# Prompt scores over 128 contraction rows: stacked key halves and doubled queries instead of four fp32 corner products

## The chip, the cores and the metric

The kernel runs on one core of one Trainium2 chip. The metric is the device time of one execution in microseconds (us), the median of several runs. Smaller is better.

## The reference, cut to what matters

One layer of a decoder: input projection, sparse attention with three branches (compressed, selected, window), a gated MLP branch, two merge projections and an output projection, for 512 prompt tokens and 8 x 4 sample tokens. The change touches the attention of the prompt. For 512 tokens all 8 selection blocks fit in the 16 that are picked and the window covers the prompt, so the selected and the window branch are both plain causal attention, each with its own keys and values:

```python
q5 = q.reshape(B, Tq, KV_HEADS, HPG, dh) * (dh ** -0.5)       # 2 key groups, 4 heads each, dh = 64
s = jnp.einsum('bqgjd,bcgd->bgjqc', q5, kc); p = masked_softmax(s, cend <= qpos)     # compressed, 31 blocks
s = jnp.einsum('bqgjd,bgqnkd->bgjqnk', q5, kg); p = masked_softmax(s, msel)          # selected
s = jnp.einsum('bqgjd,bkgd->bgjqk', q5, kw);    p = masked_softmax(s, mw)            # window
```

## The kernel before, in words

Every engine walks one common list, ORDER, written out by `plan()`, and does its own part of each entry; nothing is reordered at run time. An entry that waits holds up all later entries of that engine. SyncE (SP) and GpSimd (POOL) walk the list too and issue most DMAs.

The large projections are entries "main": one group is 24 matmuls of 128 rows by 272 or 256 columns (line 1729), three fp32r passes over 8 blocks of rows (high by high, high by low, low by high). Weights arrive in halves of a slot (`raw`); ScalarE rounds them to `w_hi` ("split", line 1046), VectorE subtracts for `w_lo` ("low", line 1313), and SP then loads the next half.

Prompt attention takes 16 units: token tile i in the order 3, 2, 1, 0 (128 queries, 128(i+1) keys: 512, 384, 256, 128 columns), branch y, and a pair of head rows jh. A unit is worked as:
- "ps" (line 2028, TensorE): scores, in two halves jj. Each half fills two banks (one for each key group g) with four fp32 matmuls of 64 rows by 64 columns of weights, one in each corner of the array. In the trace each fp32 matmul is two records, so a half is 8 records. There are three score banks.
- "ps" on VectorE (line 1611): mask and maximum of each bank.
- "px" (line 1211, ScalarE): exp; "pn" (lines 1621 and 1624 on VectorE, 1220 on ScalarE): weights and scaling; "tt" (line 1635): VectorE transposes in 32-blocks into `p_turn`, and 16 DMAs move the blocks into place, 7 issued by SP (line 837), 9 by GpSimd (line 1002).
- "pp" (line 2037): products with the values.

Beside the units, for each tile k of the compressed branch, come "cs" (line 2000, TensorE scores from `qT` and `kcp`; line 1578, VectorE), "cx", "cn", "ct" (line 2007) and "cv" (line 2014). "cs k+1" comes at the end of unit 4k+1. Between all of these stand main groups, one to a half unit. After unit 15 only projections are left, with the final norm.

Earlier in the list: the queries and keys of the prompt are turned into `qT` and `kT` ("qT", "kT", about 70 to 99 us); at 109 to 204 us the compression network; at 213 to 286 us the sample tokens' attention (`qkS`, `s_max` and so on), which uses `q_bd` and a key buffer `turned_late`.

Of the kernel before, what the change touches and what calls it, by code (L numbers as in the profile page):

```python
# [161 lines left out]
def rows_of(s):  # L162

    return ("main", s, NT, 0)
# [7 lines left out]
def plan():  # L172
# [98 lines left out]
    for c in range(1, NCH):  # L271
# [17 lines left out]
            order.append(("ln2", 0 if c == 4 else 3))  # L289
        order += ([s] if c != 7 else []) + [x for x in after if x not in (("ln", NT), ("lnr",))] + extra.get(c, [])  # L290
        turn(2)
    order += [("hidl", NCH - 1)]

    def keys(q, first, count):
        order.extend(("kt", q, k) for k in range(first, first + count))
# [5 lines left out]
    main(1)  # L301
    keys(0, 7, 5)
    main(2)
    order += [("qkS", 0)]
    for q in range(NQ):
        for n, step in enumerate(("s_max", "s_turn", "s_imp", "s_mask", "s_exp", "s_scale")):
            if step == "s_scale":
                continue
            order += [(step, q)]
            if q == 0 and n in (1, 2):  # L310
                keys(1, 3 * n - 3, 3)
            if step == "s_exp":
# [24 lines left out]

    def products(u):
        order.extend(("pp", u, kt) for kt in range(units[u][0] + 1))

    order += [("cx", 0)]
    for u in range(len(units)):
        n, k = u % 4, u // 4
        order += [("ps", u, 0)]
# [163 lines left out]
def nsa_gmlp_layer(nc, x_p, x_s, ck_cmp, cv_cmp, ck_sel, cv_sel, ck_win, cv_win, pages, w_in, w1k, w1v, w_sp,  # L508
                   w_pa, w_pb, w_o, norm_g, final_g, params, consts, outs):
    (y_p, y_s, pk_cmp, pv_cmp, pk_sel, pv_sel, pk_win, pv_win,  # L510
     sk_cmp, sv_cmp, sk_sel, sv_sel, sk_win, sv_win, s_chunk) = outs
    ctx = ExitStack()
    with ctx:
        def sb(name, shape, dt=F32):
# [2 lines left out]
        def sem(name):  # L517
            return ctx.enter_context(nc.semaphore(name))
# [40 lines left out]
        kT = placed("kT", 2048, [P, 2, TP])  # L559
        v_tok = placed("v_tok", 4096, [P, 2, NT + 1, P])  # L560
        U = placed("U", 5376, [P, 13832])
        x_hi, x_lo = placed("x_hi", 0, [P, 8, T], F32R), placed("x_lo", 4352, [P, 8, T], F32R)
# [51 lines left out]
        def sig_at(b, d):  # L614
# [51 lines left out]
        p_scored, p_bias, p_masked, p_exp, p_scaled = (sem("p_scored"), sem("p_bias"), sem("p_masked"), sem("p_exp"),  # L666
                                                       sem("p_scaled"))
        mix_ready = sem("mix_ready")
        m_sum, m_hi, m_lo = sem("m_sum"), sem("m_hi"), sem("m_lo")
        f_ssq, f_ms, f_root, f_out = sem("f_ssq"), sem("f_ms"), sem("f_root"), sem("f_out")  # L670
        f_inv, f_part, f_sum, f_out_act = sem("f_inv"), sem("f_part"), sem("f_sum"), sem("f_out_act")
# [96 lines left out]
        def _(sp):  # L768
# [43 lines left out]
            for s in ORDER:  # L812
# [7 lines left out]
                elif s == ("xt", 2, 0):  # L820
                    wait_evacuated(sp, T_AT[("qTs",)])
                    for f in range(4):
                        for a in range(4):
                            sp.dma_start(q_quarters[32 * a:32 * a + 32, f, :, :], q_bd[32 * f:32 * f + 32, :, :]).then_inc(q_spread, 16)
                elif s[0] == "load_w1":
                    sp.dma_start(w1_at[0], w1k).then_inc(w1_loaded[0], 16)
                    sp.dma_start(w1_at[1], w1v).then_inc(w1_loaded[1], 16)
                elif s[0] == "xt" and s[2] == 0 and s[1] % 5 in (1, 3):

                    for b in range(2 * n_win, 2 * n_win + 2):  # L830
                        sp.dma_start(sk_win[b, 0:512 - TQ, :], ck_win[b, TQ:512, :]).then_inc(win_out, 16)
                        sp.dma_start(sv_win[b, 0:512 - TQ, :], cv_win[b, TQ:512, :]).then_inc(win_out, 16)
                    n_win += 1
                elif s[0] == "tt" and moves_with(s[1]) == s[1]:
                    sp.wait_ge(p_turned, s[1] + 1)
                    for n in range(BY_SYNC):
                        sp.dma_start(*block_move(s[1], n)).then_inc(p_moved[s[1] % 4], 16)
                elif s[0] == "oz" and s[1] == NT - 1:

                    sp.wait_ge(p_used, len(UNITS))  # L840
                    sp.dma_start(xr[0][:, :], x_p[tok(0), :]).then_inc(xr_loaded[0], 16)
                    for j in range(4):
                        sp.dma_start(x_rows[32 * j:32 * j + 32, :, :], in_quarters(x_s)[:, j, :, :]).then_inc(xr_loaded[NT], 16)
                    sp.dma_start(pm("final_g"), final_g).then_inc(fg_loaded, 16)
                elif s[0] == "load_x":
                    i = s[1]
                    sp.wait_ge(m_lo, (4, 8, 14)[i - 1])
                    sp.dma_start(xr[i][:, :], x_p[tok(i), :]).then_inc(xr_loaded[i], 16)
                elif s[0] == "fin":
                    i = s[1]  # L850
                    k = FINS.index(i)
                    if i == NT:
                        sp.wait_ge(f_out, k + 1)
                        for j in range(4):
                            sp.dma_start(in_quarters(y_s)[:, j, :, :], x_rows[32 * j:32 * j + 32, :, :]).then_inc(y_out, 16)
# [10 lines left out]
        def _(pool):  # L866
# [97 lines left out]
            for s in ORDER:  # L964
# [7 lines left out]
                elif s[0] == "rope":  # L972
# [12 lines left out]
                    else:  # L985
                        g = s[1] - 2
                        wait_main_read(pool, last_of(f"A{g}"))
                        rope_all(512, J, G, g)
                elif s == ("ln2", NT):
                    pool.wait_ge(vn_ready, NT + 1)  # L990
                    pool.dma_start(s_chunk, vg[0:TS, NT, :]).then_inc(out_done, 16)
# [26 lines left out]
        def _(act):  # L1018
            for s in ORDER:
# [180 lines left out]
                elif kind == "ct" and t_uses(s) == ["act"]:  # L1200
                    act.wait_ge(t_done, t + 1)
                    if s[1]:
                        act.wait_ge(c_used, G * s[1])
                    nc.scalar.copy(ctb[s[2]][0:NCP, :], TB[t % 2][0:NCP, :]).then_inc(t_act, 1)
                elif kind == "px":
                    u = s[1]
                    n = (UNITS[u][0] + 1) * P
# [41 lines left out]
        def _(dve):  # L1249
# [24 lines left out]
            for s in ORDER:  # L1274
# [350 lines left out]
                elif kind == "tt":  # L1625
# [10 lines left out]
                    ins.then_inc(p_turned, 1)  # L1636
                elif kind == "oz":
                    i = TILES[s[1]]
                    dve.wait_ge(p_used, 4 * (s[1] + 1))
# [80 lines left out]
        def _(pe):  # L1720
# [11 lines left out]
            for s in ORDER:  # L1732
# [260 lines left out]
                    pe.transpose(tb[:, 0:P], o_row[:, :], ident).then_inc(t_done, 1)  # L1993
                elif kind == "cs":
                    i = TILES[s[1]]
                    if s[1] == 0:
                        wait_evacuated(pe, T_AT[("qT", NT - 1)])
                        wait_evacuated(pe, T_AT[("kT", 1)])
                    for j in range(J):
                        ins = mm(tb[:, j * 2 * NCP:(j + 1) * 2 * NCP].rearrange("p (g n) -> p g n", g=G), qT[:, j, tok(i)], kcp[:, :, :], start=True, stop=True)  # L2000
                    ins.then_inc(t_done, 1)
                elif kind == "ct":
                    i, g = s[1], s[2]
# [12 lines left out]
                elif kind == "ps":  # L2016
                    u, jj = s[1], s[2]
                    i, y, jh = UNITS[u]
                    n = (i + 1) * P
                    if u == 0 and jj == 0:  # L2020
                        pe.wait_ge(s_exp, NQ)
                    for c in range(2):
                        for g in range(G):
                            k = J * u + 2 * jj + g
                            if k >= 3 and c == 0:
                                pe.wait_ge(p_masked, k - 2)
                            r, q = slice(64 * g, 64 * g + 64), slice(i * P + 64 * c, i * P + 64 * c + 64)
                            ins = mm(S[k % 3][64 * c:64 * c + 64, 0:n], qT[r, 2 * jh + jj, q], kT[r, y, 0:n], start=True, stop=True)  # L2028
                            if c:
                                ins.then_inc(p_scored, 1)  # L2030
                elif kind == "pp":
                    u, k = s[1], s[2]
                    i, y, jh = UNITS[u]
# [71 lines left out]
```

## Time and profile before

| | us |
|---|---|
| median of 3 runs (541.36 to 541.96) | 541.64 |
| profiled execution, whole | 543.01 |
| its span in the trace | 541.3 |
| TensorE busy in the span | 523.7 (97%) |
| VectorE / ScalarE / GpSimd busy | 331.2 / 243.1 / 157.0 |

The profile is of one execution; its own time is 1.4 us above the median. A busy share is an average over stages. A matmul's duration holds its passage through the array, which overlaps with the next one, so costs on TensorE are read from start to start.

### The profile page before, as it was taken

The numbers are of one execution on the slowest core, as the hardware profiler recorded it, in microseconds if no ns is written. First come the engines' busy times: TensorE is split into PE (matmuls) and PEld (weight loads), VectorE is DVE, ScalarE is ACT, GpSimd is POOL, SyncE is SP. The second block draws the span as 40 slices with busy tenths as digits, with TensorE's granted clock in tenths as the row PEclk, the third lists the DMA queues.
The fourth block names the chain that finished last, engine by engine and source line by source line (L and its number), as shares of the span: only waits on it lengthen the run. The fifth ranks groups of instructions, "written<-read, shape, count | busy, mean of one in ns | idle before, by whom it ended". The sixth has DMA issues, their size and how long they took to land.

```text
span 541.3 us, 12831 instructions
## 1 busy us (share of the span) xinstructions
PE 523.7 (97%) x5198; PEld 473.3 (87%) x5198; DVE 331.2 (61%) x838; ACT 243.1 (45%) x564; POOL 157.0 (29%) x257
## 2 busy tenths in 40 slices
PE   6899999999999999999989999999999999999995
PEld 4899999999999998987978766767779999999995
DVE  4723231388898765674564678687753477763565
ACT  6543424534533323241241887677674432323334
POOL 0006933044414633734000066473453000000000
PEclk9999999999999999999999999999999999999998
DMA  8527652448525465877331267563454435306104
GB/s 296 214 82 218 235 181 80 154 141 290 173 61 195 142 198 168 264 282 238 101 97 40 79 155 186 148 155 100 128 140 125 131 114 155 119 1 196 40 7 161
DMA packets 59789, 81.05 MB, mean 150 GB/s; under 512 B 7825, under 2 KB 49233, under 8 KB 59218
## 3 DMA queue, kind: packets, MB, share of 16 engines
q1 hardware_dynamic: 48320, 49.97, 30.4%
q0 software_dynamic: 10688, 29.14, 17.6%
q10 hardware_dynamic: 722, 1.12, 0.6%
q8 instruction: 41, 0.67, 0.5%
q14 instruction: 18, 0.15, 0.1%
HBM read 65.23 MB, written 8.13 MB: 136 GB/s over the span
## 4 chain that ended last, share of the span: by engine, by line
PE 91%; DVE 3%; issue 2%; ACT 1%; DMA 1%; POOL 1%; DVEq 0%
PE m L1729 62%; PE so L2028 4%; PE so L2037 3%; PE so L1900 3%; PE so L1903 3%; PE so L1901 3%; PE m L1813 2%; PE so L1939 2%; PE so L1877 1%; PE so L1988 1%; DMA U<-p_turn 1%; PE t L1865 1%; POOL U L1002 1%; PE t L1755 1%; PE so L1742 1%
## 5 line engine op out<-in xcount | busy, mean ns | idle before, releaser
L1729 PE MATMUL m<-h_hi,w_hi 128*128 128x272 f32 x448 | 132.7, 296 | 1.0 <-DVE za L1426 0.8
L1729 PE MATMUL m<-h_hi,w_lo 128*128 128x272 f32 x448 | 129.2, 288 | 0.0
L1729 PE MATMUL m<-h_lo,w_hi 128*128 128x272 f32 x448 | 128.7, 287 | 0.0
L1729 PE MATMUL m<-w_hi,h_hi 128*128 128x256 f32 (+2 forms) x360 | 104.1, 289 | 2.4 <-issue 1.9
L1729 PE MATMUL m<-w_hi,h_lo 128*128 128x256 f32 (+2 forms) x360 | 101.9, 283 | 0.0
L1729 PE MATMUL m<-w_lo,h_hi 128*128 128x256 f32 (+2 forms) x360 | 101.9, 283 | 0.0
L1313 DVE TENSOR_TENSOR w_lo<-raw,w_hi 128x1024 fp32r<-128x1024 f32 (+2 forms) x62 | 71.0, 1155 | 42.6 <-ACT w_hi L1046 42.5
L1729 PEld LDWEIGHTS m<-h_hi,w_hi 128*128 128x128 f32 x448 | 84.3, 188 | 13.4 <-issue 10.2
L1002 POOL DMA_DIRECT2D U<-p_turn x108 | 58.2, 547 | 104.0 <-DVE p_turn L1635 102.6
L1729 PEld LDWEIGHTS m<-h_hi,w_lo 128*128 128x128 f32 x448 | 84.5, 189 | 0.0
L1729 PEld LDWEIGHTS m<-h_lo,w_hi 128*128 128x128 f32 x448 | 84.4, 188 | 0.0
L1729 PEld LDWEIGHTS m<-w_hi,h_hi 128*128 128x128 f32 (+1 forms) x360 | 67.8, 188 | 3.9 <-issue 2.1
L1729 PEld LDWEIGHTS m<-w_lo,h_hi 128*128 128x128 f32 (+1 forms) x360 | 68.0, 189 | 0.1
L1729 PEld LDWEIGHTS m<-w_hi,h_lo 128*128 128x128 f32 (+1 forms) x360 | 67.8, 188 | 0.1
L1046 ACT CAST w_hi<-raw 128x1024 fp32r<-128x1024 f32 (+2 forms) x62 | 60.9, 990 | 1.0 <-DMA raw<-in_w_in 0.5
L1611 DVE CUSTOM_DVE_ANT_0 U<-so,cst 128x512 f32<-128x512 f32 (+3 forms) x64 | 28.7, 485 | 20.2 <-PE so L2028 20.2
L1220 ACT ACTIVATE U<-U,st 128x512 f32<-128x512 f32 (+3 forms) x64 | 30.7, 551 | 18.9 <-DVE st L1624 18.9
L1729 PE MATMUL m<-x_hi,w_lo 128*128 128x272 f32 x128 | 37.0, 289 | 0.0
L1729 PE MATMUL m<-x_hi,w_hi 128*128 128x272 f32 x128 | 36.8, 288 | 0.0
L1729 PE MATMUL m<-x_lo,w_hi 128*128 128x272 f32 x128 | 36.7, 287 | 0.0
L1211 ACT ACTIVATE U<-U,st 128x512 f32<-128x512 f32 (+3 forms) x64 | 35.1, 551 | 2.9 <-DVE st L1615 2.9
L1900 PE MATMUL so<-xt_sb,w_hi 128*128 128x256 f32 x128 | 32.0, 290 | 0.2 <-ACT xt_sb L1161 0.2
(301 smaller groups left out, 904.3 us busy)
## 6 DMA issues: line engine op xcount, KB each, us to landing
raw<-in_w_in SPq DMA_DIRECT2D x36, 512.0 KB
U<-in_x_p SPq DMA_DIRECT2D x8, 512.0 KB, 5.9
raw<-in_w_o SPq DMA_DIRECT2D x8, 512.0 KB
U<-p_turn POOLq DMA_DIRECT2D x54, 64.0 KB, 2.6
U<-p_turn SPq DMA_DIRECT2D x42, 64.0 KB, 2.8
raw<-in_w_in SPq DMA_DIRECT2D x8, 256.0 KB
raw<-in_w_pa SPq DMA_DIRECT2D x8, 256.0 KB
raw<-in_w_pb SPq DMA_DIRECT2D x4, 512.0 KB
```

The lines of the kernel that those rows point to most:

```text
L1002: pool.dma_start(*block_move(s[1], n)).then_inc(p_moved_pool[s[1] % 4], 16)
L1046: ins = nc.scalar.copy(hi, x)
L1211: ins = nc.scalar.activation(pb[u][:, j, 0:n], pb[u][:, j, 0:n], ACT.Exp, bias=st[:, m + 4 + j:m + 5 + j], scale=SCALE, accum_out=st[:, m ...
L1220: ins = nc.scalar.activation(pb[u][:, j, 0:n], pb[u][:, j, 0:n], ACT.Copy, scale=st[:, m + 12 + j:m + 13 + j])
L1313: ins = v.tensor_tensor(lo, x, hi.bitcast(F32), ALU.subtract)
L1611: v.tensor_tensor_reduce(pb[u][:, a, 0:n], S[k % 3][:, 0:n], cs("causal")[:, 512 - n:512], 1.0, -3e38, ALU.add, ALU.max, st[:, m + a:m + a ...
L1729: ins = mm(out, lhs(a, k), rhs(b, k), start=(k == 0 and a + b == 0), stop=(k == n - 1 and a == 1))
L1900: mm(out[:, 0:256], w, x(xt_hi), start=(j == 0), stop=False, skip_group_check=True)
L1901: ins = mm(out[:, 0:256], w1_lo[:, j, :], x(xt_hi), start=False, stop=False, skip_group_check=True)
L1903: ins = mm(out[:, 0:256], w, x(xt_lo), start=False, stop=(j == 15), skip_group_check=True)
L2028: ins = mm(S[k % 3][64 * c:64 * c + 64, 0:n], qT[r, 2 * jh + jj, q], kT[r, y, 0:n], start=True, stop=True)
L2037: ins = mm(O[64 * g:64 * g + 64, 256 * jh:256 * jh + 256].rearrange("p (j a r) -> p j a r", j=2, a=4), v_tok[:, y, k, g * DH:(g + 1) * DH] ...
```

## The change

The high part (fp32r rounding) and the low part (remainder) of the keys are stacked to 128 rows in `k_st`: for group g the high part on rows 64g to 64g+63, the low part on the other 64. The queries are stored on both halves of the partitions ("doubled"), split into `q_h` and `q_l`, and each bank of scores is made by two full-array fp32r matmuls, 128 rows by 128 queries, over 128(i+1) key columns. `k_st` lies where `qT` was, so the queries go out to DRAM (`q_dram`) and come back for each pair of units; `cs` reads its plain queries back too, into `h_rows` and `q_bd`. New entries of the list:
- "ks": ScalarE two copies, VectorE two subtractions (64 x 1024), GpSimd two DMAs, ahead of "hidl 9".
- "ql m": ScalarE issues two DMAs for unit pair m. "qh m": ScalarE copies 128 x 512, VectorE subtracts 128 x 512.
- "qc k": GpSimd issues four DMAs of 64 KB for `cs k`.

The order of units within a tile becomes head pair outside, branch inside. The core of the diff:

```diff
-    order += [("hidl", NCH - 1)]
+    order += [("ks",), ("hidl", NCH - 1)]
...
-    order += [("qkS", 0)]
+    order += [("ql", 0), ("qkS", 0)]
...
+            if q == NQ - 1 and n == 0:
+                order += [("qc", 0)]
...
-            order += [("s_out", q), ("qkS", 1)]
+            order += [("s_out", q), ("qkS", 1), ("qh", 0)]
...
-    units = [(i, y, jh) for i in TILES for y in range(2) for jh in range(2)]
+    units = [(i, y, jh) for i in TILES for jh in range(2) for y in range(2)]
...
-    order += [("cx", 0)]
+    order += [("ql", 1), ("cx", 0)]
...
         if u:
             order += [("pn", u - 1)]
+            if u % 2 and m < len(units) // 2:
+                order += [("qh", m)]
...
             order += [("ct", k, 0), ("ct", k, 1)]
+            if k < NT - 1:
+                order += [("qc", k + 1)]
         order += [("px", u)]
+        if u % 2 and m + 1 < len(units) // 2:
+            order += [("ql", m + 1)]
...
+                elif s[0] == "qTs":
+                    for i in range(NT):
+                        wait_evacuated(sp, T_AT[("qT", i)])
+                    for g in range(G):
+                        sp.dma_start(q_dram[:, :, g, :], qT[64 * g:64 * g + 64, :, :]).then_inc(q_saved, 16)
...
+                elif s[0] == "qc":
+                    i = TILES[s[1]]
+                    if s[1]:
+                        pool.wait_ge(t_done, T_AT[("cs", s[1] - 1)] + 1)
+                    else:
+                        pool.wait_ge(qk_done, NQ)
...
+                    for n in range(2):
+                        for g in range(G):
+                            pool.dma_start(q_plain[n][64 * g:64 * g + 64, :, :], q_dram[:, 2 * n:2 * n + 2, g, tok(i)]).then_inc(q_plain_loaded, 16)
+                elif s[0] == "ks":
+                    pool.wait_ge(k_lo_done, 1)
+                    for g in range(G):
+                        a, b = slice(64 * g, 64 * g + 64), slice(64 - 64 * g, 128 - 64 * g)
+                        pool.dma_start(k_st[b, g, :, :], k_lo[a, :, :]).then_inc(k_moved, 16)
...
+                elif kind == "ql":
...
+                    for a in (slice(0, 64), slice(64, 128)):
+                        nc.scalar.dma_start(q_f[m % 2][a, :, :], src).then_inc(q_loaded[m % 2], 16)
+                elif kind == "qh":
+                    m = s[1]
+                    act.wait_ge(q_loaded[m % 2], 32 * (m // 2 + 1))
+                    nc.scalar.copy(q_h[m % 2][:, :, :], q_f[m % 2][:, :, :]).then_inc(q_hi_done, 1)
...
+                elif kind == "qh":
+                    m = s[1]
+                    dve.wait_ge(q_hi_done, m + 1)
+                    v.tensor_tensor(q_l[m % 2][:, :, :], q_f[m % 2][:, :, :], q_h[m % 2][:, :, :].bitcast(F32), ALU.subtract).then_inc(q_lo_done, 1)
...
-                    for c in range(2):
-                        for g in range(G):
-                            k = J * u + 2 * jj + g
-                            if k >= 3 and c == 0:
-                                pe.wait_ge(p_masked, k - 2)
-                            r, q = slice(64 * g, 64 * g + 64), slice(i * P + 64 * c, i * P + 64 * c + 64)
-                            ins = mm(S[k % 3][64 * c:64 * c + 64, 0:n], qT[r, 2 * jh + jj, q], kT[r, y, 0:n], start=True, stop=True)
-                            if c:
-                                ins.then_inc(p_scored, 1)
+                    for g in range(G):
+                        k = J * u + 2 * jj + g
+                        if k >= 3:
+                            pe.wait_ge(p_masked, k - 2)
+                        for x in (q_h, q_l):
+                            ins = mm(S[k % 3][:, 0:n], x[m % 2][:, 2 * jj + g, :], k_st[:, g, y, 0:n], start=(x is q_h), stop=(x is q_l))
+                        ins.then_inc(p_scored, 1)
```

## Rows read from the trace of the kernel before

**Rows 1.** The page, busy time: us, share of the span, instructions.
```profile
PE 523.7 (97%) x5198; PEld 473.3 (87%) x5198; DVE 331.2 (61%) x838; ACT 243.1 (45%) x564; POOL 157.0 (29%) x257
```

**Rows 2.** Windows, 312 to 344 us: stretch, us, busy by engine PE, PEld, DVE, ACT, POOL.
```profile
312.00:344.00 32.00, 31.98 (x242) 21.89 (x241) 23.63 (x67) 24.15 (x54) 20.16 (x38) 1.00 0.66 168
```

**Rows 3.** Timeline of TensorE, 302.6 to 304.1 us: start, us.
```profile
302.63 0.29 PE L1729 MATMUL m<-h_hi,w_lo 128*128 128x272 f32 x1
302.85 1.09 PE L2028 MATMUL so<-kT,qT 64*64 64x512 f32 x8
303.87 0.39 PE L1729 MATMUL m<-h_hi,w_hi 128*128 128x272 f32 x1
304.10 0.29 PE L1729 MATMUL m<-h_lo,w_hi 128*128 128x272 f32 x1
```

**Rows 4.** Chain of work that ended last: start, us, what, records.
```profile
307.16 0.84 PE t L2000 x8
...
333.70 0.81 PE so L2028 x8
...
391.13 0.38 PE so L2028 x8
...
420.83 66.14 PE m L1729 x528
...
520.52 14.37 PE m L1729 x120
```

**Rows 5.** Timelines of VectorE, ScalarE and GpSimd; idle time before each in brackets.
```profile
200.80 0.47 ACT L1173 ACTIVATE U<-so,prm 128x256 f32<-128x256 f32 x1 [6.27 <-PE so L1903]
...
204.16 0.44 DVE L1413 TENSOR_TENSOR sg<-sg,tmp 128x272 f32<-128x272 f32 x1 [3.87 <-issue]
...
255.78 0.22 DVE L1492 TENSOR_REDUCE st<-so 128x1 f32<-128x63 f32 x1 [2.69 <-PE so L1946]
...
200.98 0.94 POOL L943 DMA_INDIRECT turned_late<-in_ck_sel,half_rows  x1 [7.02 <-PE so L1903]
```

**Rows 6.** Timelines of VectorE and ScalarE, unit 1, and two like operations.
```profile
191.81 1.89 DVE L1450 TENSOR_TENSOR xt_sb<-U,xt_sb 128x512 fp32r<-128x512 f32 x3
...
302.73 0.17 DVE L1624 TENSOR_TENSOR st<-st,gate 128x4 f32<-128x4 f32 x1
302.81 1.22 DVE L1313 TENSOR_TENSOR w_lo<-raw,w_hi 128x1024 fp32r<-128x1024 f32 x1
...
307.88 2.48 DVE L1635 STREAM_TRANSPOSE p_turn<-U 128x512 f32<-128x512 f32 x4
310.29 0.38 DVE L1578 TENSOR_TENSOR U<-t,cst 128x248 f32<-128x248 f32 x1
...
311.48 0.68 DVE L1611 CUSTOM_DVE_ANT_0 U<-so,cst 128x512 f32<-128x512 f32 x1
...
238.75 0.60 ACT L1196 COPY U<-t 128x512 f32<-128x512 f32 x1
...
302.93 2.56 ACT L1220 ACTIVATE U<-U,st 128x512 f32<-128x512 f32 x4 [0.45 <-DVE st L1624]
```

**Rows 7.** Chain, scores of units 2 and 3.
```profile
312.23 1.86 PE so L2028 x10
```

**Rows 8.** Timeline of GpSimd: issues of the block moves after unit 3 and unit 7.
```profile
335.00 4.87 POOL L1002 DMA_DIRECT2D U<-p_turn  x9 [1.75 <-DVE p_turn L1635]
...
366.26 4.84 POOL L1002 DMA_DIRECT2D U<-p_turn  x9 [1.74 <-DVE p_turn L1635]
```

**Rows 9.** Line 1002: time from a move's issue to its landing.
```profile
DMA to landing us min/median/max: 1.7/2.3/5.7
```

**Rows 10.** Chain, the compressed scores of tiles 2 and 3.
```profile
343.63 1.03 PE t L2000 x8
...
371.30 1.03 PE t L2000 x8
```

**Rows 11.** Windows near the end: busy by engine, granted clock, DMA share, GB/s.
```profile
537.00:538.00 1.00, 0.00 (x0) 0.00 (x0) 0.93 (x4) 0.69 (x1) 0.00 (x0) 0.50 0.70 260
```

More of the change, by code:

```diff
@@ L339, in products @@
         order.extend(("pp", u, kt) for kt in range(units[u][0] + 1))
-    order += [("cx", 0)]
+    order += [("ql", 1), ("cx", 0)]
     for u in range(len(units)):
         n, k = u % 4, u // 4
+        m = u // 2 + 1
         order += [("ps", u, 0)]
@@ L511, in nsa_gmlp_layer @@
      sk_cmp, sv_cmp, sk_sel, sv_sel, sk_win, sv_win, s_chunk) = outs
+    q_dram = nc.dram_tensor("q_dram", (DH, J, G, TP), F32, kind="Internal").ap()
     ctx = ExitStack()
@@ L559, in nsa_gmlp_layer @@
         kT = placed("kT", 2048, [P, 2, TP])
+        k_st = placed("k_st", 0, [P, G, 2, TP], F32R)
+        k_lo = placed("k_lo", 2048, [P, 2, TP], F32R)
+        q_f = [placed(f"q_f{n}", 2048 + 1024 * n, [P, J, P]) for n in range(2)]
+        q_l = [placed(f"q_l{n}", 2048 + 1024 * n, [P, J, P], F32R) for n in range(2)]
+        q_h = [placed(f"q_h{n}", 2560 + 1024 * n, [P, J, P], F32R) for n in range(2)]
+        q_plain = [x[:, :, :].rearrange("p k t -> p (k t)").rearrange("p (j n) -> p j n", j=2) for x in (h_rows, q_bd)]
         v_tok = placed("v_tok", 4096, [P, 2, NT + 1, P])
@@ L668, in nsa_gmlp_layer @@
         mix_ready = sem("mix_ready")
+        q_saved, k_hi_done, k_lo_done, k_moved = sem("q_saved"), sem("k_hi_done"), sem("k_lo_done"), sem("k_moved")
+        q_loaded, q_hi_done, q_lo_done = [sem("q_loaded0"), sem("q_loaded1")], sem("q_hi_done"), sem("q_lo_done")
+        q_plain_loaded = sem("q_plain_loaded")
         m_sum, m_hi, m_lo = sem("m_sum"), sem("m_hi"), sem("m_lo")
@@ L988, in _ @@
                         rope_all(512, J, G, g)
+                elif s[0] == "qc":
[4 more added lines that the diff above has]
+                        pool.wait_ge(qk_done, NQ)
+                        pool.wait_ge(main_done, MAIN_AT[rows_of(SLOT["V1"])] + 1)
+                        pool.wait_ge(q_saved, 32)
+                    for n in range(2):
[6 more added lines that the diff above has]
+                        pool.dma_start(k_st[b, g, :, :], k_lo[a, :, :]).then_inc(k_moved, 16)
                 elif s == ("ln2", NT):
@@ L1204, in _ @@
                     nc.scalar.copy(ctb[s[2]][0:NCP, :], TB[t % 2][0:NCP, :]).then_inc(t_act, 1)
+                elif kind == "ks":
+                    for y in range(2):
+                        wait_evacuated(act, T_AT[("kT", y)])
+                    act.wait_ge(q_saved, 32)
+                    for g in range(G):
+                        r = slice(64 * g, 64 * g + 64)
+                        ins = nc.scalar.copy(k_st[r, g, :, :], kT[r, :, :])
+                    ins.then_inc(k_hi_done, 1)
+                elif kind == "ql":
+                    m = s[1]
+                    i, _, jh = UNITS[2 * m]
+                    if m == 0:
+                        act.wait_ge(k_moved, 32)
+                    elif m == 1:
+                        act.wait_ge(o_done, NQ)
+                    else:
+                        act.wait_ge(p_scored, 2 * J * (m - 1))
+                    src = q_dram[:, 2 * jh:2 * jh + 2, :, tok(i)].rearrange("d j g t -> d (j g) t")
+                    for a in (slice(0, 64), slice(64, 128)):
[4 more added lines that the diff above has]
+                    nc.scalar.copy(q_h[m % 2][:, :, :], q_f[m % 2][:, :, :]).then_inc(q_hi_done, 1)
                 elif kind == "px":
@@ L1636, in _ @@
                     ins.then_inc(p_turned, 1)
+                elif kind == "ks":
+                    dve.wait_ge(k_hi_done, 1)
+                    for g in range(G):
+                        r = slice(64 * g, 64 * g + 64)
+                        ins = v.tensor_tensor(k_lo[r, :, :], kT[r, :, :], k_st[r, g, :, :].bitcast(F32), ALU.subtract)
+                    ins.then_inc(k_lo_done, 1)
+                elif kind == "qh":
+                    m = s[1]
+                    dve.wait_ge(q_hi_done, m + 1)
+                    v.tensor_tensor(q_l[m % 2][:, :, :], q_f[m % 2][:, :, :], q_h[m % 2][:, :, :].bitcast(F32), ALU.subtract).then_inc(q_lo_done, 1)
                 elif kind == "oz":
@@ L1995, in _ @@
                     i = TILES[s[1]]
-                    if s[1] == 0:
-                        wait_evacuated(pe, T_AT[("qT", NT - 1)])
-                        wait_evacuated(pe, T_AT[("kT", 1)])
+                    pe.wait_ge(q_plain_loaded, 16 * 4 * (s[1] + 1))
                     for j in range(J):
-                        ins = mm(tb[:, j * 2 * NCP:(j + 1) * 2 * NCP].rearrange("p (g n) -> p g n", g=G), qT[:, j, tok(i)], kcp[:, :, :], start=True, stop=True)
+                        ins = mm(tb[:, j * 2 * NCP:(j + 1) * 2 * NCP].rearrange("p (g n) -> p g n", g=G), q_plain[j // 2][:, j % 2, :], kcp[:, :, :], start=True, stop=True)
                     ins.then_inc(t_done, 1)
@@ L2019, in _ @@
                     n = (i + 1) * P
+                    m = u // 2
                     if u == 0 and jj == 0:
                         pe.wait_ge(s_exp, NQ)
-                    for c in range(2):
-                        for g in range(G):
-                            k = J * u + 2 * jj + g
-                            if k >= 3 and c == 0:
-                                pe.wait_ge(p_masked, k - 2)
-                            r, q = slice(64 * g, 64 * g + 64), slice(i * P + 64 * c, i * P + 64 * c + 64)
-                            ins = mm(S[k % 3][64 * c:64 * c + 64, 0:n], qT[r, 2 * jh + jj, q], kT[r, y, 0:n], start=True, stop=True)
-                            if c:
-                                ins.then_inc(p_scored, 1)
+                        pe.wait_ge(k_moved, 32)
+                    if u % 2 == 0 and jj == 0:
+                        pe.wait_ge(q_hi_done, m + 1)
+                        pe.wait_ge(q_lo_done, m + 1)
+                    for g in range(G):
+                        k = J * u + 2 * jj + g
[4 more added lines that the diff above has]
+                        ins.then_inc(p_scored, 1)
                 elif kind == "pp":
```

## The prediction

> **What bounds the kernel now.** I read the page's busy shares first: TensorE is busy 97% of the span, the next engine 61% [rows 1]. Then windows over the stage of the prompt scores: of the 32 us from 312 TensorE is busy 31.98, VectorE 23.63, ScalarE 24.15, GpSimd 20.16 [rows 2]. So what is taken from TensorE's queue here shortens the run, and every wait put into that queue lengthens it by its full length: after unit 15 it has only projections, 528 matmuls in a row in 66.14 us [rows 4], in which nothing can be made up. But VectorE and ScalarE have only about a quarter of their time left, and both work their lists strictly in order. The chain shows that they do bind once already: a stretch of scores takes 1.86 us [rows 7] where 10 records at 1.02 us for 8 would take 1.3. So the next views were the timelines of VectorE, ScalarE and GpSimd between 286 and 409 us, entry by entry against ORDER.
>
> **TensorE's own work.** A half unit of 512 columns takes 1.02 us from its start (302.85) to the next main group's (303.87); 384 columns take 0.81 and 128 take 0.38 [rows 3, 4]. That is 1.67 ns per column, four cycles of 2.4 GHz for all four corners together, plus 0.17; 256 columns give 0.59. Around it, the matmul before starts 0.22 ahead of it instead of 0.125, and the first main matmul after it holds 0.23 instead of 0.125 [rows 3, 4]: 0.10 us to enter the cornered form and 0.11 to leave it.
> Afterwards a half is four full-array fp32r matmuls. Main matmuls of 272 columns come every 66.14/528 = 125.3 ns [rows 4], which is 113.3 of columns plus 12. So 512 columns: 4 x (213.3 + 12) = 0.90 us; 384: 0.69; 256: 0.48. The streaming is the same four cycles per column as before; only the fixed parts differ. For 128 columns no row has an fp32r matmul so narrow. Lower end: 4 x (53.3 + 12) = 0.26. Upper end: the fp32 rate of four cycles per column, 4 x 213 = 0.85. The nearest row in shape is a full-array weight load with 62 columns behind it, 0.84 us for 8 records, 105 ns each [rows 4], so 0.43 is taken.
> Eight halves of each width: 8 x (-0.12 - 0.12 - 0.11 + 0.05) = -2.4 us. By ORDER, 20 halves are entered from a full-array neighbour and 23 left to one: 20 x 0.10 + 23 x 0.11 = 4.5 us gone. In their place 10 are now entered from a cornered or half-width neighbour ("pp", "cv", the sample values) and 7 left to one: 1.8 us new. Sum -5.1 us; with the ends of the 128-column price -6.4 to -1.7.
> On these borders a rule of the Trainium skill bears, page "TensorEngine Tiling (Array Packing)", section "Key Properties": changing the tiling mode drains TensorE, changing the tile within a mode does not. The trace agrees (0.22 against 0.125). By the page alone, whose tiles multiply throughput, giving up four concurrent 64 x 64 tiles should cost; by the rows it costs nothing, since fp32r needs a quarter of fp32's cycles. Without the drains the sum would be -2.4.
>
> **Parts ahead of the stage: nothing.** "ks": ScalarE's two copies and VectorE's two subtractions of 64 x 1024, about 1.1 us each, fall ahead of 200.80 and 204.16, where these engines sat idle 6.27 and 3.87 us; GpSimd's two DMAs fall in its idle 7.02 us [rows 5]. Without that cover the sample keys would come late and TensorE would wait up to 4 us before the sample scores. "qh 0": VectorE has 2.69 us idle ahead of 255.78 [rows 5], the subtraction takes 0.63. Storing the queries (1 MB) puts SP's later loads back by some 3 us at about 103 us, where they are prefetches. "ql 0" and "qc 0" have over 20 us each until their use. I keep 0, with up to +1 for the range.
>
> **The query split in the odd units.** "qh m" stands right behind "pn" of the even unit. On ScalarE that means behind the four scalings, 302.93 to 305.49 in unit 1, then its own copy, 0.6 us [rows 6]: done at 306.0. VectorE meets "qh 1" at 302.9, directly after its last weight operation, and can't pass it: it stands for 3.1 us and then needs 0.63 (three like subtractions take 1.89) [rows 6]. Behind it in VectorE's queue stand, in this order, a "low", two masks, a second "low", the transposes of unit 0, "cs 1" and the masks of unit 2, for which TensorE waits through its three score banks. From 306.6: low 1.2, masks 1.3 (0.68 each, less an overlap), bias 0.2, low 1.2, transposes 2.4, cs 1.2 [rows 6] give 314.1 for the first mask of unit 2 instead of 311.48, 2.6 us late, done at 314.7. The last bank of unit 2 needs that mask; TensorE is there at about 312.0 and stands 2.5 us. "qh 2" in unit 3 does the same again. Walking the four queues through units 2 to 4 in this way, with each entry's own duration, I get 5.8 us of TensorE waits where the same walk of the kernel before has 1.4: +4.4 us. The walk of the kernel before reaches the last product of the stage within 0.3 us of the trace. Later ones (units 5 to 13) mostly find VectorE ahead, because of the next item; they add 1.2 us around unit 8 and 1.3 us around units 12 to 14. ScalarE's 14 extra issues and 7 copies are inside this walk. Bounds: 0 if VectorE had its work done, and 7 x 3.7 = 26 if nothing hid any.
>
> **The reload for the compressed scores.** "qc 2" stands in GpSimd's queue behind the nine block moves after unit 3, "qc 3" behind the nine after unit 7. TensorE's "cs 2" and "cs 3" now wait for them; before they waited for nothing. In the timing before, the moves after unit 7 are issued from 366.26 to 371.10 [rows 8]. Four more issues at 0.54 each: the last starts at 372.7 and lands 2.3 us later (the median of the moves) [rows 8, 9], at 375.0. TensorE reaches "cs 3" at 371.30 [rows 10], and about 0.7 us earlier relative to unit 8 by its own savings: a wait of some 4.4 us. For "cs 2" likewise: moves 335.00 to 339.87, landing at 343.8, TensorE at 343.63 [rows 8 to 10]: 1 us. To this comes that the transposes which release the moves sit late on VectorE through "qh": in the walk by 1.5 us more at either place, giving 2.7 and 6.0 us, 8.7 together. All that stands behind "cs" on TensorE waits too, the main groups among it. Bounds: 5.4 if VectorE isn't late; 8.7 + 2 x 3 = 15 if both landings take the longest of the moves, 5.7 us [rows 9].
>
> **Sum.** -5.1 + 4.4 + 1.2 + 1.3 + 8.7 = +10.5 us on an execution of 543.0, 553.5; the runs shown have their median 1.4 lower, so 552.0.
>
> **Rivals.**
> (a) Only the work saved counts: both reloads land in time and VectorE takes the splits in its gaps. Then -5.1, less about 1 us because VectorE already binds at units 2 and 3: 537.5, faster. For it: VectorE is idle a quarter of the stage. Against it: the idle time lies behind entries that wait for TensorE, and GpSimd's 4.84 us of issues ahead of "qc 3" are in the trace.
> (b) One of the two waits only. Without the "qh" effect the walk gives +3.5, without the "qc" effect +4: 545. It decides if the copies on ScalarE come earlier than I think, or if TensorE has enough ahead of "cs".
> (c) TensorE's clock falls in the 6 us wait. At the end of the run its last group ends at 534.9 [rows 4], and the window from 537 shows 0.50, that is 1.2 GHz [rows 11]. So a gap like that before "cs 3" is long enough. If 3 to 5 us of work follow at half clock, +1.5 to +2.5: 554. The Trainium skill's page "TensorE: Matmul & The Clock Gate", section "Part 1: The HAM clock gate", says that idleness halves the clock and that renewed work restores it; the first half agrees with the trace, the way back no row shows.
> (d) 128 columns run at the upper end, 8 x 0.42 = +3.4: 555.
>
> **How the numbers follow.** My sum 0.45, (b) 0.20, (c) 0.13, (d) 0.10, (a) 0.12. The likeliest gives 552.0. (a) lies on the faster side, and with it comes a strip of (b): faster 0.12, same 0.03, slower 0.85, where about 0.2% is what this kernel's runs can tell from no change. The range leaves out (a) and the far end of the landings: 543.5 to 558.
>
> **What would show it.** Right: TensorE waits of 4 to 7 us ahead of line 2000 in tile 0 or 1's compressed scores, released by a DMA that GpSimd issued; VectorE idle some 3 us before each subtraction of the queries, released by ScalarE; halves of 512 columns at 0.90 us; main groups of 3.01 us next to them. Wrong: "cs" with no wait, or TensorE over 96% busy between 286 and 421 us; a wait near 204 to 214 us for `k_moved` or late keys would mean that I mis-priced "ks".

## The result, and the profile after

| | before | after |
|---|---|---|
| median, us (4 runs each) | 541.55 (541.36 to 541.96) | 561.59 (561.30 to 563.53) |
| ratio to before, 95% interval | 1 | 1.036 (1.033 to 1.039) |
| profiled execution / its span | 543.01 / 541.3 | 561.73 / 560.0 |
| prompt attention: start of the first score to start of the last product group | 286.26 to 419.82 = 133.6 | 287.70 to 438.52 = 150.8 |

The change costs 3.6%, 20 us. The forecast was 552.0 us with a range to 558: the direction and the two causes of waiting were right, the size was not.

Of the 18.7 us between the two spans, 17.2 lie in the prompt attention. The other 1.5 come at 16 to 24 us, long before anything that was changed (told at the end).

The page after; this line answers to [rows 1]:

```profile
PE 528.7 (94%) x5070; PEld 492.7 (88%) x5070; DVE 338.1 (60%) x848; ACT 249.5 (45%) x574; POOL 168.5 (30%) x275
```

TensorE has 128 instructions fewer and is busy 5 us *longer*, at a lower share. Work taken out and yet more busy time: the same work must have run slower. The windows say where: first those of before, then after (columns as in [rows 2], with the granted clock, the DMA share and GB/s last).

```profile
346.00:376.00 30.00, 30.00 (x254) 21.70 (x252) 23.52 (x79) 22.46 (x60) 15.39 (x29) 1.00 0.50 125
376.00:406.00 30.00, 29.15 (x270) 22.02 (x268) 20.71 (x91) 21.97 (x73) 14.35 (x27) 1.00 0.53 138
```

```profile
316.00:346.00 30.00, 29.57 (x204) 24.49 (x205) 22.15 (x63) 24.25 (x54) 19.04 (x36) 0.94 0.69 181
346.00:376.00 30.00, 25.96 (x181) 21.44 (x178) 20.55 (x61) 18.80 (x51) 15.61 (x30) 0.94 0.58 142
376.00:406.00 30.00, 22.22 (x141) 19.43 (x140) 17.18 (x65) 16.16 (x47) 12.06 (x22) 0.83 0.50 123
```

Two things are new: TensorE stands (22.22 of 30 us where it was 29.15), and its clock is below 1.00 in these three windows. From 284 to 316 and from 406 to 436 us it is 1.00, and before in all five. The clock has two levels, 1.2 and 2.4 GHz, so a mean of 0.83 over 30 us is a third of the time at the lower one. What was lost to it is (1 - clock) x length: (0.06 + 0.06 + 0.17) x 30 = 8.7 us. Up to 0.8 of it cost nothing: from 384.00 to 385.85 the clock is 0.58 while TensorE still waits.

TensorE's waits between 286 and 440 us, by what ended them (us in total, times, longest). Before, to the end of its stage, then after:

```profile
PE so L2037 <- DMA U<-p_turn: 0.6, 1, 0.6
PE so L2028 <- DVE st L1611: 0.2, 1, 0.2
```

```profile
PE t L2072 <- DMA q_bd<-q_dram: 9.9, 2, 6.6
PE so L2104 <- DVE st L1675: 4.7, 6, 1.9
PE so L2112 <- DMA U<-p_turn: 0.3, 1, 0.3
PE so L2104 <- issue: 0.2, 1, 0.2
```

15.1 us against 0.8. The first line is the reload of `cs`, the second the masks of the score banks. Both are in the chain of work that ended last. Around unit 1 it now runs through ScalarE and VectorE; before, through TensorE [rows 7]:

```profile
304.66 1.93 ACT U L1284 x3
306.59 0.52 ACT q_h L1268
307.13 0.69 DVE q_l L1710
307.83 1.13 DVE w_lo L1377
...
311.51 2.40 DVE p_turn L1699 x4
...
315.02 0.68 DVE U L1675
```

ScalarE's scalings, its copy of the queries, VectorE's subtraction, everything queued behind that, and only at 315.02 the mask that TensorE's third bank needs; before it was at 311.48 [rows 6]. The timelines of VectorE and TensorE show the wait at either end (idle time in brackets):

```profile
307.13 0.69 DVE L1710 TENSOR_TENSOR q_l<-q_f,q_h 128x512 fp32r<-128x512 f32 x1 [3.14 <-ACT q_h L1268]
```

```profile
315.77 0.58 PE L2104 MATMUL so<-k_st,q_h 128*128 128x512 f32 x1 [1.93 <-DVE st L1675]
```

And the chain around `cs 3`, which before was entered from TensorE's own work at 371.30 [rows 10]:

```profile
378.44 2.70 POOL U L1042 x5
381.13 1.17 POOL h_rows L1023 x2
382.30 0.56 POOL q_bd L1023
382.87 2.85 DMA q_bd<-q_dram
...
385.85 1.94 PE t L2072 x8
387.79 0.96 PE so L2104 x4
388.75 4.13 PE m L1803 x24
```

Block moves, four more issues behind them, the landing, then TensorE. Now read durations: the eight records of `cs` take 1.94 us where they took 1.03, and a main group of 24 matmuls 4.13 where it takes 3.01 at full clock. That is work at 1.2 GHz after the wait, for the greater part of both. In windows of 4 us:

```profile
380.00:384.00 4.00, 0.00 (x0) 0.00 (x0) 2.31 (x10) 2.67 (x9) 3.46 (x7) 1.00 0.71 164
384.00:388.00 4.00, 2.15 (x10) 2.18 (x11) 0.17 (x1) 0.00 (x0) 0.00 (x0) 0.54 0.21 41
388.00:392.00 4.00, 4.00 (x23) 4.00 (x23) 3.15 (x10) 1.71 (x4) 0.00 (x0) 0.61 0.00 0
```

But the long waits are not the only ones that cost clock. After the 1.93 us at 315.77 it reads:

```profile
312.00:316.00 4.00, 2.07 (x14) 1.63 (x14) 3.93 (x10) 1.35 (x4) 1.80 (x4) 1.00 0.87 231
316.00:320.00 4.00, 4.00 (x16) 3.12 (x16) 2.73 (x11) 3.35 (x6) 3.11 (x6) 0.57 0.79 194
```

TensorE is busy throughout the second window and gets 16 records done; in the window after it, at 1.00, 29.

### The profile page after: what moved, and what is told of

Its sections match the earlier page's. It is cut to its first block, busy times and chain, and to the rows that moved or that the text cites. A ratio compares the mean times of both kernels' runs of the same rounds, so it can differ in the third digit from the quotient of the medians.

```text
span 560.0 us, 12647 instructions
## 1 busy us (share of the span) xinstructions
PE 528.7 (94%) x5070; PEld 492.7 (88%) x5070; DVE 338.1 (60%) x848; ACT 249.5 (45%) x574; POOL 168.5 (30%) x275
## 4 chain that ended last, share of the span: by engine, by line
PE 76%; DVE 10%; ACT 5%; POOL 3%; issue 3%; DMA 3%; DVEq 0%
PE m L1803 53%; PE so L1974 3%; PE so L1977 3%; DVE p_turn L1699 3%; PE so L1975 3%; POOL U L1042 3%; ACT U L1284 2%; DVE U L1675 2%; PE m L1887 2%; PE so L2013 1%; DVE w_lo L1377 1%; PE so L2104 1%; PE so L1951 1%; DMA q_bd<-q_dram 1%; PE so L2062 1%
## 5 line engine op out<-in xcount | busy, mean ns | idle before, releaser
L1803 PE MATMUL m<-h_hi,w_lo 128*128 128x272 f32 x448 | 130.4, 291 | 0.0
L1803 PE MATMUL m<-h_lo,w_hi 128*128 128x272 f32 x448 | 130.2, 291 | 0.0
L1803 PEld LDWEIGHTS m<-h_hi,w_hi 128*128 128x128 f32 x448 | 86.1, 192 | 3.7 <-issue 1.8
L1803 PEld LDWEIGHTS m<-h_lo,w_hi 128*128 128x128 f32 x448 | 86.1, 192 | 0.3
L1803 PEld LDWEIGHTS m<-h_hi,w_lo 128*128 128x128 f32 x448 | 85.9, 192 | 0.0
```

The costliest lines, as they stand in the source:

```text
L1803: ins = mm(out, lhs(a, k), rhs(b, k), start=(k == 0 and a + b == 0), stop=(k == n - 1 and a == 1))
```

## The experiments

One theory runs through them: the stage's length is 133.6 us, less 5.1 us for TensorE's own work saved, plus its waits beyond the 0.8 of before, plus what the lower clock takes. The 5.1 is the forecast, not a measurement. What tells the theories apart stands in this table, which the sections below explain (us; stage from first score to last product as above; waits from 284 or 286 us on; clock loss from windows of about 30 us; sum = 128.5 + waits - 0.8 + clock loss, for the three kernels of the old form 133.6 in place of 128.5):

| kernel | ratio to before | waits | clock loss | sum | stage measured |
|---|---|---|---|---|---|
| before | 1 | 0.8 | 0 | 133.6 | 133.6 |
| changed | 1.036 | 15.1 | 8.7 | 151.5 | 150.8 |
| 1 query split early | 1.016 | 10.2 | 5.1 | 143.0 | 142.8 |
| 2 reload early | 1.010 | 6.4 | 4.9 | 139.0 | 139.5 |
| 3 both early | 0.9955 | 2.7 | 0 | 130.4 | 130.8 |
| 4 waits filled (+8.8 of idle work) | 1.026 | 8.2 | 1.8 | 146.5 | 148.2 |
| 5 changed again | 1.031 | 15.9 | 9.9 | 153.5 | 152.6 |
| 6 only the copy early | 0.993 | 2.7 | 0 | 130.4 | 130.6 |
| 7 both early, mains spread | 0.988 | 1.5 | 0 | 129.2 | 128.7 |
| 8 before with a reload wait | 1.009 | 5.2 | 1.5 | 139.5 | 139.6 |
| 9 before, mains spread | 0.997 | 1.0 | 0 | 133.8 | 132.4 |
| 10 as 7, again | 0.991 | 1.2 | 0 | 128.9 | 128.3 |

The sum is off by up to 1.7 us. In 9 it is 1.4 too high, because the list of waits leaves out a stretch in which TensorE counts as busy: the ten records in 1.86 us of [rows 7] become eight in 1.09 when unit 2 has another main group ahead of its mask.

Since the median of the kernel before was 540.6, 544.5 and 542.2 us in the three sets of runs, the ratios are what is to be compared, and beside them the stages of the profiles. The microseconds of whole executions mislead. In the twelve profiles the first score starts anywhere from 283.0 to 288.1 us: from 283.0 to 284.6 in experiments 1 to 4, and at 287.6 and 288.0 in the two of the changed kernel. From the start of the last product group to the end it is the same 121.5 us in all twelve.

### 1. The query split a unit earlier

```diff
-            if u % 2 and m < len(units) // 2:
-                order += [("qh", m)]
...
+        if u % 2 == 0 and m < len(units) // 2:
+            order += [("qh", m)]
         order += [("px", u)]
```

> The query split of pair m stands a unit earlier, ahead of the exp of the even unit, instead of behind its scalings. Theory (queue order, then clock): VectorE no longer stands 3 us for ScalarE in every odd unit; TensorE's waits before scores fall from 4.7 us to about 3, and cs 3 still waits 4 to 5 us for GpSimd's reload. By the walk 7 us less than the changed kernel, by its fewer clock falls some 3 more: 551 to 555 us. Rival (the full-array form itself slows or throttles TensorE): within 2 us of the changed kernel, 560 to 562, clock 0.98 as there.

Measured: 549.12 us (548.73 to 551.72), ratio 1.016 (1.012 to 1.020). Waits for masks fell from 4.7 to 2.5 us, those for the reload from 9.9 to 7.2, since the transposes that release the moves come sooner; the clock loss from 8.7 to 5.1. In the stage that saves 8.0 us, where 7 of walk and some 3 of clock were expected: a wait removed gives its clock back too. That the time lies below my range comes from ahead of the stage, where this execution's first score starts 4.7 us sooner.

### 2. The reload issued right behind the `cs` before it

```diff
-            if k < NT - 1:
-                order += [("qc", k + 1)]
+            if k == 0:
+                order += [("qc", 1)]
...
+            if n == 1 and k < NT - 2:
+                order += [("qc", k + 2)]
```

The first of these stands behind "ct", the second behind "cs k+1".

> The reload for the next compressed scores is issued right behind the ones before it, four units of GpSimd moves earlier; the query split stays. Theory (queue order, then clock): the two waits of TensorE at its compressed scores (3.3 and 6.6 us) are gone, the waits for VectorE stay or grow: by the walk 6.5 us less, with the clock falls behind them 8 to 12 less: 550 to 554 us. Rival (form itself): 560 to 562.

Measured: 546.98 us (545.49 to 547.38), ratio 1.010 (1.007 to 1.013). `cs` waits for nothing any more:

```profile
PE so L2106 <- DVE st L1677: 4.5, 6, 1.9
PE so L2106 <- ACT q_h L1270: 1.9, 1, 1.9
```

The time is below my range for the same reason as in 1; the stage is 11.3 us shorter, where 8 to 12 were expected. But the clock still falls, though no single wait is over 1.94 us. Windows and the waits inside them:

```profile
308.00:312.00 4.00, 2.40 (x18) 1.97 (x16) 3.93 (x9) 1.92 (x6) 1.23 (x3) 1.00 0.91 259
312.00:316.00 4.00, 3.66 (x11) 2.76 (x12) 2.73 (x12) 2.78 (x6) 4.00 (x8) 0.60 0.83 197
```

```profile
312.34 0.50 PE L2106 MATMUL so<-k_st,q_h 128*128 128x512 f32 x1 [1.94 <-DVE st L1677]
...
384.69 0.45 PE L2106 MATMUL so<-k_st,q_h 128*128 128x128 f32 x1 [1.87 <-ACT q_h L1270]
```

At the second place the wait is for ScalarE's copy, and 0.77 us for a mask follow at 386.12. So waits of under 2 us can pull the clock down on their own. They don't always do it: see 5.

### 3. Both

The two edits together.

> Both moves. Theory: no reload wait, VectorE waits about 3 us in all, no clock fall in the stage: the walk gives 3.5 us less than before, 538 us (536 to 541). If only one of the two placements mattered: about that one's time, 550 or more. Rival (form itself slows or throttles): at least 550.

Measured: 538.36 us (537.58 to 539.54, 8 runs), ratio 0.9955 (0.9935 to 0.9975), as expected, and faster than before. The clock is 1.00 in every window from 284 to 436 us, and the waits left are

```profile
PE so L2106 <- DVE st L1677: 2.5, 3, 1.5
PE so L2114 <- DMA U<-p_turn: 0.2, 1, 0.2
```

The arithmetic of the change was good all along; the stage is 2.8 us shorter with 1.9 us more of waits, so TensorE's own work is 4.7 us less. Undoing one delay saves 2.0 or 2.6 points of ratio (8.0 or 11.3 us of the stage), undoing both 4.0 points (20.0 us).

### 4. The waits filled with idle matmuls

The changed kernel, with 22 and 48 matmuls of 272 columns, whose results nobody reads, ahead of the waits of `cs 2` and `cs 3`.

```diff
+                    for _ in range((0, 0, 22, 48)[s[1]]):
+                        mm(tb[:, 0:272], h_hi[:, 0, 0:P], h_hi[:, 1, 0:272], start=True, stop=True)
```

> The changed kernel with TensorE given 22 idle matmuls of 272 columns (2.8 us) ahead of its wait for the reload in cs 2 and 48 (6.0 us) ahead of the one in cs 3; their result is overwritten. More work, all of it inside waits. Theory with the clock: the clock no longer falls after these waits, 3 to 6 us less than the changed kernel (555 to 558). If the clock fall costs nothing, or has another cause: 0 to 1 us more than the changed kernel (561 to 563).

Measured: 554.61 us (554.15 to 556.98), ratio 1.026 (1.022 to 1.030), for 70 matmuls more; the changed kernel has 1.036, and 1.031 (1.027 to 1.035) in experiment 5. The 7 us between the medians overstate the effect: of 6.9 us between the spans (553.1 and 560.0) 4.2 lie ahead of the first score. The stage is 2.7 us shorter. The waits for the reload shrank, the clock came back:

```profile
PE so L2106 <- DVE st L1675: 5.8, 8, 1.9
PE t L2074 <- DMA q_bd<-q_dram: 2.2, 2, 1.3
```

```profile
346.00:376.00 30.00, 28.64 (x212) 23.74 (x213) 21.06 (x68) 19.81 (x50) 17.32 (x33) 1.00 0.57 139
376.00:406.00 30.00, 27.89 (x206) 24.72 (x205) 18.11 (x69) 17.51 (x56) 10.56 (x20) 0.94 0.48 120
```

`cs 3` starts 98.2 us behind the first score with and without the idle work, since it waits for GpSimd either way; what the clock gave back behind `cs 2` was waited away there. From the start of `cs 3` to the last product group it is 49.9 us instead of 52.6. These 2.7 us isolate the clock: no dependency and no transfer was changed. The clock loss is 1.8 us instead of 8.7, but 1.7 of the difference is the fall at 316 us, ahead of the first idle matmul (342.3); the same wait of 1.94 us stands here at 311.56 and the clock stays at 1.00.

### 5. The changed kernel again

Unaltered, as a control beside 6 to 8.

> The changed kernel once more, unaltered, beside the others of this call, as the control: 560 to 563 us. Its first profile had the clock at 0.69 between 20 and 24 us, which the other kernels did not; if that belongs to the change it is there again, if it is chance it is not, and the time is nearer to 560.

Measured: 562.41 us (559.12 to 563.87), ratio 1.031 (1.027 to 1.035). The waits for the reload repeat (9.9 us), and so does the dip at 16 to 24 us; the clock loss is much the same (9.9 us for 8.7), but not every fall stands where it stood. The wait of unit 2 is as long as before, and this time no fall comes behind it:

```profile
316.17 0.50 PE L2104 MATMUL so<-k_st,q_h 128*128 128x512 f32 x1 [1.94 <-DVE st L1675]
```

```profile
316.00:320.00 4.00, 3.66 (x20) 2.83 (x21) 2.73 (x12) 2.95 (x6) 3.53 (x7) 1.00 0.78 191
```

So one program, with one and the same wait, loses clock there in one execution and not in the next; behind `cs 3` it loses it in both.

### 6. Only ScalarE's copy early

The reload early as in 2. Of the query split only ScalarE's copy goes a unit earlier (a new entry "qa"); VectorE's subtraction stays behind "pn".

```diff
+        if u % 2 == 0 and m < len(units) // 2:
+            order += [("qa", m)]
...
-                elif kind == "qh":
+                elif kind == "qa" or s == ("qh", 0):
```

(the second is in ScalarE's part)

> With the early reload, only ScalarE's copy of the query split goes a unit earlier; VectorE's subtraction stays behind the weights of the even unit, as in the change. Theory: what costs is that VectorE stands behind ScalarE's scalings and copy, not the subtraction's 0.6 us there: the walk gives 4 us less than before, 537 to 540 us, as with both entries moved. Rival (VectorE's place and load decide): halfway to the kernel with the early reload alone, 542 to 546.

Measured: 541.21 us (539.18 to 541.73), ratio 0.993 (0.990 to 0.995). The time in microseconds lies above the range that I gave, but so did the kernel before in this set; by the ratio (0.993 x 541.6 = 537.8) it is inside, and within the intervals equal to 3. VectorE's timeline has no gap ahead of the subtraction:

```profile
304.26 0.17 DVE L1692 TENSOR_TENSOR st<-st,gate 128x4 f32<-128x4 f32 x1
304.34 0.68 DVE L1714 TENSOR_TENSOR q_l<-q_f,q_h 128x512 fp32r<-128x512 f32 x1
```

The subtraction itself, 0.68 us, costs nothing where it stands. What cost was that VectorE stood 3.14 us for a copy that ScalarE does after its scalings.

### 7. Both early, main groups spread differently

As 3, with the number of main groups in units 2 and 5 exchanged, so that unit 2 has more work ahead of its mask.

```diff
-AFTER_FIRST_SCORES, AFTER_SCORES = 2, [1, 2, 1, 2, 1, 2, 1, 1, 1, 1, 1, 1, 1, 1, 1, 1]
+AFTER_FIRST_SCORES, AFTER_SCORES = 2, [1, 2, 2, 2, 1, 1, 1, 1, 1, 1, 1, 1, 1, 1, 1, 1]
```

> Both placements mended and one main group more between the scores of units 2 and 3, one fewer in unit 5. Theory: the 2.5 us that TensorE still waits there fall to about 1; the walk gives 2 to 2.5 us less than with both placements mended: 535.5 to 537. Rival (the waits are covered by nothing else and reappear at the products' moves): 538 to 539.

Measured: 538.24 us (537.77 to 539.99), ratio 0.988 (0.987 to 0.990). In microseconds that is above what I gave; by the ratio (0.988 x 541.6 = 535.1) it is just below it; the same kernel in 10 has 0.991, which makes 536.7 and is inside. The waits for masks are 0.9 us, the stage 128.7.

### 8. The kernel before with a reload wait

The old scores, old `qT` and nothing of the change but this: GpSimd issues four DMAs of 64 KB at the places of "qc", and `cs` waits for them.

```diff
+            if k < NT - 1:
+                order += [("qc", k + 1)]
...
+                    else:
+                        pe.wait_ge(reload_sem, 16 * 4 * s[1])
```

> The kernel before, fp32 corner products and all, with one part of the change alone: GpSimd issues four 64 KB DMAs at the place of qc 1, 2 and 3 (into memory that is free by then), and the compressed scores wait for them; what is loaded isn't used. Theory: waits of about 1 and 4 us at cs 2 and cs 3, and a clock fall behind the second: 546 to 549 us. If the clock falls only with the new form of the scores: 545 to 546. If the wait weren't GpSimd's queue but the change's own data: 541.5.

Measured: 548.83 us (548.36 to 550.22), ratio 1.009 (1.007 to 1.011). That is inside the range that I gave. The wait costs 4.3 us between the medians and 6.0 in the stage, and takes the clock along:

```profile
PE t L2012 <- DMA h_rows<-in_x_p: 3.7, 2, 3.5
```

```profile
372.00:376.00 4.00, 1.59 (x12) 1.36 (x16) 0.34 (x1) 0.64 (x4) 0.80 (x2) 0.90 0.16 31
376.00:380.00 4.00, 4.00 (x27) 3.39 (x20) 2.98 (x10) 1.71 (x4) 0.00 (x0) 0.67 0.00 0
```

So the falling clock is not a property of the new full-array matmuls. That these draw the lower clock by themselves is excluded here, and by 3 and 7, which have them at 1.00. Without the late VectorE, GpSimd's queue alone makes 3.5 us of wait at `cs 3`, against the 4.4 that the prediction had for this part.

### 9 and 10. Is it the spread or the change?

The kernel before with the list of 7 (the counts of units 2 and 5 are what differs; the expectation words that loosely), and 7 once more beside it.

> The kernel before, with only the number of main groups behind the second halves of units 3 to 5 changed (2, 2, 1 instead of 1, 2, 2... as in the version with the early entries: list 1, 2, 2, 2, 1, 1). Theory 1: the gain of the early version over the kernel before is the four full-array matmuls' own, and the spread of the main groups only takes a wait for masks away that the kernel before hardly has (0.2 us, and 0.6 us for block moves): 0 to -0.8 us, ratio 0.998 to 1.000. Rival: the spread itself brings what that version gained over the early one, about 2 to 4 us: ratio 0.993 to 0.996.

> The early version with spread main groups once more, beside the kernel before with the same spread: ratio to the kernel before 0.986 to 0.993, and 4 to 6 us below the kernel before with the spread alone if theory 1 holds; equal to it within 2 us if the rival does.

Measured: 541.79 us (540.03 to 542.65, 12 runs), ratio 0.997 (0.996 to 0.999), and 537.83 us (536.65 to 538.48, 6 runs), ratio 0.991 (0.989 to 0.993). The spread gives the old kernel 0.3%, a little more than the 0 to 0.2% of theory 1; on top of it the change, with its entries early, is worth 4.0 us. That is at the lower edge of what theory 1 gave, and the best kernel here is the changed one with three edits in its list: 0.9 to 1.2% faster than before, where the change as made is 3.6% slower.

## Why the prediction was wrong in size

- **TensorE's own work, -5.1: right, a little high.** -4.7 by experiment 3 (against before); -4.2 by 7 and -4.3 by 10 against 9, which has the same spread (stages 128.7 and 128.3 for 132.4, waits 1.5 and 1.2 for 1.0). A half of 512 columns takes 0.93 us, forecast 0.90: in experiment 3 the four matmuls start at 291.76, 291.99, 292.22 and 292.46, the next main group at 292.69. Neither border costs anything. For 128 columns I took 0.43 between 0.26 and 0.85; the rows give 0.48 and 0.52 for two halves, so rival (d) is refuted:

```profile
413.14 0.22 PE L2104 MATMUL so<-k_st,q_h 128*128 128x128 f32 x1
413.20 0.28 PE L2104 MATMUL so<-k_st,q_l 128*128 128x128 f32 x1
413.31 0.27 PE L2104 MATMUL so<-k_st,q_h 128*128 128x128 f32 x1
413.42 0.27 PE L2104 MATMUL so<-k_st,q_l 128*128 128x128 f32 x1
413.62 0.30 PE L2104 MATMUL so<-k_st,q_h 128*128 128x128 f32 x1
...
414.14 0.34 PE L1803 MATMUL m<-h_hi,w_hi 128*128 128x272 f32 x1
```

- **Parts ahead of the stage, 0: right.** TensorE's waits between 200 and 286 us are the same four as before, 2.5 us against 2.6.
- **The query split, +4.4 +1.2 +1.3: right in kind, a little high.** VectorE stands 3.14 us where 3.1 was forecast. The first mask of unit 2 comes at 315.02; with the stage's start 1.4 us later, that is 2.1 us late against 2.6. The waits for masks are 4.7 us in six places, where 6.9 was expected in all. In experiments 3 and 6, where it is gone, 2.5 and 1.9 us remain; the sum has no term for them, and rival (a) allowed about 1 us.
- **The reload, +8.7 (2.7 and 6.0): right, a little low.** 9.9, the two being 3.3 and 6.6.
- **The sum of waits: right.** 15.6 forecast, 14.3 more than before measured. With the work saved this makes +9.2 us, where the prediction had +10.5.
- **The failed step: the clock.** The likeliest case had nothing for it. Rival (c), "TensorE's clock falls in the 6 us wait", saw one fall, for 3 to 5 us of work: +1.5 to +2.5. The runs show 8.7 us lost, in falls behind both `cs` waits (1.94 us for 1.03; 4.13 for 3.01), behind a mask wait of 1.93 us, and once more at 400 to 404 us (0.67), at a mask wait of 1.02 us. I had looked for one gap as long as that at the run's end [rows 11], which showed a clock already fallen and not how short a gap is enough. The window before it in the same trace does show that, with the last matmul ended at 534.9:

```profile
536.00:537.00 1.00, 0.00 (x0) 0.00 (x0) 0.66 (x5) 0.20 (x1) 0.00 (x0) 0.92 0.72 258
```

  Here the clock fell some 2 us after the last matmul (in the other eleven profiles 2.2 to 5.2 us after it). The term to put into the sum would have been one for the waits together: 8.7 us of clock to 15.1 of waiting in the changed kernel (0.6, and again 0.6 in 5), 0.5 and 0.8 for each microsecond waited in experiments 1 and 2, 0.3 in experiment 8, 0.2 in 4, and nothing in 3, 6, 7, 9 and 10 with 1.0 to 2.7 us of waits in all.
- **The start-up, not in any forecast.** 1.5 us of this execution's 18.7 (below).

The Trainium skill bears on the failed step: the page "TensorE: Matmul & The Clock Gate", section "A second HAM failure mode: psum-queue depth-cycling", tells of a kernel whose small idle times between groups of matmuls make the clock go up and down. Experiment 2 agrees, with 1.94 us as its longest wait and the clock at 0.60 behind it. The prediction had weighed only that page's part on long idleness.

Rival (a), savings only, is what experiments 3, 6 and 7 reach once both delays are taken out; for the change as made it is refuted, and (b) with it, as both waits were there. The two figures of (b), +3.5 and +4, don't follow from the terms of my sum, which give about +0.3 without the query split (-5.1 + 5.4) and +1.8 without the reload. Experiments 1 and 2 have one of the two each: their stages are 9.2 and 5.9 us longer than before, 4.1 and 1.0 without the clock.

## What to carry to other kernels

Where TensorE is the bound and its clock falls behind waits, a wait can cost more than its own length, 0.2 to 0.8 more here where waits came to 5 us or more in all, and nothing where they came to 2.7 or less. Sum the waits, then add a range for the clock: for waits of 1 to 2 us it starts at nothing, behind unfilled ones of 2.7 us and more these runs always lost some. Before cheaper arithmetic is put into a strictly ordered list, look at what each new entry stands behind: the copy belongs ahead of the engine's long job and the reload ahead of the burst of moves, and here three such edits turned +3.6% into about -1%. If a kernel got slower with fewer instructions and *more* busy time on its bounding engine, read the clock column of the windows first.

## What the hardware showed that I had not expected

- The clock of TensorE fell after waits of 1.9 us (0.57 and 0.60 in the 4 us that follow). But the length of the longest wait doesn't decide it. The wait of 1.94 us left the clock at 1.00 in experiments 4 and 5, and experiments 1 and 3 have one of 1.49 us that did too. A mask wait of 1.02 us, on the other hand, had a fall with it or within 2 us behind it in the changed kernel and in experiments 4 and 5; one of 1.02 us for block moves in experiment 8 had none. Single waits of 2.7 us and more inside the stage lost clock in every profile that has them unfilled. What else decides, and how much it depends on where the wait lies in time, stays open.
- Filling the waits with matmuls that nobody reads shortened the stage by 2.7 us against leaving TensorE idle.
- At 16 to 24 us, in the input phase with the same work in all, some executions lose clock: 0.88 and 0.69 in the two windows of the changed kernel's profile, 1.00 and 1.00 before.

```profile
16.00:20.00 4.00, 2.13 (x15) 1.92 (x14) 2.21 (x3) 4.00 (x7) 0.00 (x0) 0.88 1.03 414
20.00:24.00 4.00, 4.00 (x27) 4.00 (x26) 3.39 (x10) 1.96 (x6) 0.64 (x1) 0.69 0.25 89
```

  The profiles of experiments 5, 6 and 7 have it too, those of before, 1 to 4 and 8 to 10 do not. It does not follow the program: 7 and 10 are the same one, with the dip and without. It comes behind a wait of 1.87 us that ends at 18.6 us, and before has the same wait (1.86), as experiments 4 and 8 do (1.87), with the clock at 1.00. Why it comes in one execution and not in another stays open.
- A full-array matmul on fp32r data of 128 columns starts mostly 0.11 to 0.16 us after the one before it, in the eight rows from 413.14 (one pair is 0.06 apart). That is more than its columns by the rate of the wide ones (53.3 + 12 ns), and its lower end is close to the 105 ns of a full weight load with 62 columns behind it [rows 4].
